# A hybrid decoder layer on one core: 16 of the 22 up steps of each feed-forward computed as seven block products

## The chip, the cores and the metric
The kernel runs on one core of one Trainium2 chip. The metric is the device time of one launch in microseconds; the time before is 1206.61 us, the median of three runs (1205.77 to 1208.55).

## The reference
The layer is a feed-forward, a token mixer and a second feed-forward, each between RMS norms, for 512 tokens of width 1024. The change touches only the feed-forwards:

```python
def rms_norm(x, g):
    xf = x.astype(jnp.float32)
    y = xf * lax.rsqrt(jnp.mean(xf * xf, axis=-1, keepdims=True) + EPS)
    return (y * g.astype(jnp.float32)).astype(x.dtype)
...
def swiglu(x, w_gu, w_down):
    g, u = jnp.split(x @ w_gu, 2, axis=-1)
    return (jax.nn.silu(g) * u) @ w_down
```

Here w_gu is 1024 by 5632 (2816 gate columns, 2816 up columns) and w_down is 2816 by 1024, all float32.

## The kernel before
**Work and tiles.** One feed-forward is 22 up steps and 11 down steps. An up step takes 128 gate and 128 up columns of w_gu, 1 MB of weights, as 8 row blocks of 256 columns, and multiplies them with the normed x, held transposed (`xn`, 8 blocks of 128 rows by 512 tokens). A down step takes 256 rows of w_down, also 1 MB.

**Precision.** Every float32 operand is split into a rounded part (hi) and the rest (lo), and a product is three matmuls: hi by hi, hi by lo, lo by hi (`MODES`). So an up step is 8 blocks, 2 output tiles and 3 modes, 48 matmuls of 128x128 by 512 columns; a down step is 48 as well.

**The weight ring.** SyncE's queue loads step n into `ring_raw` slot n % 2, as two transfers of 512 KB (`load`). ACT copies it to `ring_hi` (`hi`, L670), VectorE subtracts to give `ring_lo` (`lo`, L946) and signals `lo_ready`; the load of step n waits until `lo` of step n-2 is done. ACT's copy waits for the matmuls of step n-2 (`w_used`), since there are two slots of `ring_hi` and `ring_lo`.

**After an up step**, VectorE multiplies gate and up sums by the norm's factor `rb` (L1024, L1025), ACT takes the silu (L734), VectorE multiplies (L1028), ACT rounds (L738) and VectorE subtracts (L1033), which gives `hT_hi` and `hT_lo` for the down steps. Each engine runs its instructions in the order of the program, and a wait holds all that is behind it on that engine.

**GpSimd (POOL)** builds the attention bias tables while the first up steps run: a memset and copies into `bias_vec` (L551, L560), a store (L563), five broadcasts to DRAM (L571); later it adds y to x (`add_x`, L585).

## Time and profile before

| what | value |
|---|---|
| median of 3 runs | 1206.61 us |
| profiled execution, device time | 1207.43 us |
| its span in the trace | 1205.7 us |
| PE busy / VectorE / ACT / POOL | 99% / 44% / 33% / 7% |
| granted TensorE clock, mean | 0.999 |
| data moved | 123.19 MB, mean 102 GB/s |

The time of the profiled execution is 1.7 us more than its span. "Busy" of PE counts overlapping matmuls once; the pitch of matmuls is read from the start of one to the start of the next, or from a piece of the chain divided by its count, not from the duration of one.

### The profile page before, as it was taken

What the parts mean: (1) busy time and instruction counts of PE and PEld (TensorE: products, weight loads), DVE (VectorE), ACT (ScalarE), POOL (GpSimd) and SP (SyncE); (2) the same over time, 40 slices, a digit from 0 to 9 for tenths busy, and PEclk for the clock granted to TensorE, in tenths of its full rate; (3) what the DMA queues carried; (4) which work ended last, traced back from release to release, by engine and by line L of the source; (5) the groups of instructions that cost most, each with busy time, mean ns of one, the idle gap of its engine ahead of it and who ended that gap; (6) DMA issues with size and microseconds to landing.
All of it is one profiled execution on the core that took longest, in us unless ns stands there. A gap on an engine that the chain in (4) does not pass through costs nothing.

```text
span 1205.7 us, 15537 instructions
## 1 busy us (share of the span) xinstructions
PE 1188.7 (99%) x6054; PEld 986.2 (82%) x6054; DVE 535.2 (44%) x806; ACT 399.0 (33%) x643; POOL 86.8 (7%) x198
## 2 busy tenths in 40 slices
PE   9999999999999999999999999999999999999998
PEld 7888888888887888998777788887888888888886
DVE  3444444431226435436776343646444444442223
ACT  5222222221125211246676313325422222221113
POOL 7000000000005100000031100002000000000002
PEclk9999999999999999999999999999999999999999
DMA  7843333232225343371200232332333333333321
GB/s 207 263 113 96 104 104 87 87 123 105 105 87 145 96 118 104 108 242 36 73 3 2 70 105 70 123 105 70 101 90 88 104 104 96 83 115 107 105 70 70
DMA packets 138511, 123.19 MB, mean 102 GB/s; under 512 B 4180, under 2 KB 125180, under 8 KB 138444
## 3 DMA queue, kind: packets, MB, share of 16 engines
q1 hardware_dynamic: 134272, 108.02, 29.7%
q0 software_dynamic: 4080, 14.50, 3.7%
q8 instruction: 32, 0.52, 0.2%
q14 instruction: 15, 0.12, 0.0%
q10 hardware_dynamic: 112, 0.03, 0.0%
HBM read 118.08 MB, written 8.90 MB: 105 GB/s over the span
## 4 chain that ended last, share of the span: by engine, by line
PE 93%; DVE 2%; DMA 2%; ACT 1%; issue 1%; SPq 0%; DVEq 0%; ACTq 0%
PE ps L1369 53%; PE ps L1453 20%; PE ps L1556 4%; PE ps L1824 4%; PE ps L1622 2%; PE ps L1611 2%; DMA ring_raw<-in_ffn_w_gu 2%; PE ps L1808 2%; PE ps L1679 2%; PE ps L1657 1%; PE ps L1796 1%; PE ps L1393 1%; ACT ring_hi L670 1%; DVE ring_lo L946 1%; DMA x_tok<-in_x 0%
## 5 line engine op out<-in xcount | busy, mean ns | idle before, releaser
L1369 PE MATMUL ps<-xn_hi,ring_hi 128*128 128x512 f32 x992 | 388.7, 392 | 2.9 <-DVE ring_lo L946 1.6
L1369 PE MATMUL ps<-xn_hi,ring_lo 128*128 128x512 f32 x992 | 386.2, 389 | 0.0
L1369 PE MATMUL ps<-xn_lo,ring_hi 128*128 128x512 f32 x992 | 386.1, 389 | 0.0
L946 DVE TENSOR_TENSOR ring_lo<-ring_raw,ring_hi 128x2048 fp32r<-128x2048 f32 (+1 forms) x89 | 201.8, 2268 | 255.5 <-ACT ring_hi L670 255.5
L670 ACT ACTIVATE ring_hi<-ring_raw 128x2048 fp32r<-128x2048 f32 (+1 forms) x89 | 167.9, 1888 | 255.1 <-PE ps L1453 157.6
L1369 PEld LDWEIGHTS ps<-xn_hi,ring_hi 128*128 128x128 f32 x992 | 186.2, 188 | 42.7 <-issue 4.3
L1369 PEld LDWEIGHTS ps<-xn_hi,ring_lo 128*128 128x128 f32 x992 | 186.2, 188 | 39.1
L1369 PEld LDWEIGHTS ps<-xn_lo,ring_hi 128*128 128x128 f32 x992 | 186.3, 188 | 37.7
L1453 PE MATMUL ps<-ring_hi,hT_hi 128*128 128x512 f32 x352 | 136.9, 389 | 0.0
L1453 PE MATMUL ps<-ring_hi,hT_lo 128*128 128x512 f32 x352 | 136.9, 389 | 0.0
L1453 PE MATMUL ps<-ring_lo,hT_hi 128*128 128x512 f32 x352 | 136.9, 389 | 0.0
L734 ACT ACTIVATE silu_g<-silu_g 128x512 f32<-128x512 f32 x44 | 27.8, 632 | 324.4 <-DVE silu_g L1024 324.4
L1024 DVE TENSOR_TENSOR silu_g<-ps,rb 128x512 f32<-128x512 f32 x44 | 30.4, 691 | 187.1 <-PE ps L1369 187.0
L1453 PEld LDWEIGHTS ps<-ring_hi,hT_lo 128*128 128x128 f32 x352 | 66.1, 188 | 13.8
L1453 PEld LDWEIGHTS ps<-ring_hi,hT_hi 128*128 128x128 f32 x352 | 66.1, 188 | 13.7
L1453 PEld LDWEIGHTS ps<-ring_lo,hT_hi 128*128 128x128 f32 x352 | 66.1, 188 | 13.7
L957 DVE TENSOR_TENSOR ring_lo<-ring_raw,ring_hi 128x1024 fp32r<-128x1024 f32 x22 | 26.0, 1221 | 51.2 <-ACT ring_hi L680 51.1
L585 POOL TENSOR_TENSOR x_tok<-y_gained,x_tok 128x512 f32<-128x512 f32 x18 | 22.7, 1281 | 291.2 <-DVE y_gained L999 291.2
L836 ACT ACTIVATE p_n<-s_sb,stat_m 128x128 f32<-128x128 f32 (+2 forms) x64 | 35.3, 552 | 18.4 <-DVE stat_m L1175 18.4
L1556 PE MATMUL ps<-ring_hi,xn_hi 128*128 128x256 f32 x128 | 36.5, 285 | 0.7 <-DVE ring_lo L957 0.7
L680 ACT ACTIVATE ring_hi<-ring_raw 128x1024 fp32r<-128x1024 f32 x22 | 22.1, 1051 | 44.3 <-PE ps L1556 16.1
L1556 PE MATMUL ps<-ring_lo,xn_hi 128*128 128x256 f32 x128 | 36.2, 283 | 0.0
(232 smaller groups left out, 1161.6 us busy)
## 6 DMA issues: line engine op xcount, KB each, us to landing
ring_raw<-in_ffn_w_gu SPq DMA_DIRECT2D x86, 512.0 KB, 5.0
ring_raw<-in_ffn_w_down SPq DMA_DIRECT2D x44, 512.0 KB, 4.0
ring_raw<-in_w_in SPq DMA_DIRECT2D x44, 512.0 KB, 4.7
ring_raw<-in_w_out SPq DMA_DIRECT2D x8, 512.0 KB, 4.3
bias_rows_sparse<-bias_by_distance POOLq DMA_DIRECT2D x1, 2560.0 KB, 15.5
x_tok<-in_x SPq DMA_DIRECT2D x8, 256.0 KB, 5.3
ring_raw<-in_cmp_w_k SPq DMA_DIRECT2D x4, 512.0 KB, 4.4
ring_raw<-in_cmp_w_v SPq DMA_DIRECT2D x4, 512.0 KB, 4.5
```

The costliest lines, as they stand in the source:

```text
L670: e = act.activation(dst, src, ACT.Copy)
L734: act.activation(silu_g[:, u, :], silu_g[:, u, :], ACT.Silu).then_inc(act_read, 1)
L836: e = act.activation(p_of(u)[:, c0:c1], s_sb[:, u % 2, c0:c1], ACT.Exp, bias=least, scale=-1.0, accum_out=den)
L946: e = dve.tensor_tensor(dst, src, f32(r), ALU.subtract)
L957: return dve.tensor_tensor(dst, src, f32(r), ALU.subtract)
L1024: dve.tensor_tensor(silu_g[:, u, :], ps[:, 2 * slot, :], rb[:, :], ALU.mult).then_inc(g_scaled, 1)
L1369: e = pe.matmul(ps[:, 2 * (slot if pair is None else pair) + c, :], part(a, slot, k * 256 + c * P, P), xn[b][:, k, :], start=(k == 0 and i ...
L1453: e = pe.matmul(ps[:, j, :], hT[b][:, tokens], part(a, ring_slot(n0), kk * D + c * S, S), start=(n == 0 and kk == 0 and q == 0), stop=(n = ...
L1556: e = pe.matmul(ps[:, V_BANK[i][t // 2], (t % 2) * 256:(t % 2) * 256 + 256], xn[b][:, k, tokens], part(a, ring_slot(n), k * 256, 256), sta ...
L1611: e = pe.matmul(ps[:, (u + half) % 4, c0:c1], q, k, start=True, stop=True)
L1622: e = pe.transpose(ps[:, 4 + u % 2, x * P:x * P + P], p_of(u)[:, x * P:x * P + P], ident[:, :])
L1824: e = pe.matmul(ps[:, 2 * t + c, :], xn[b][:, k, t * P:t * P + P], part(a, ring_slot(n), kk * D + c * S, S), start=(k == 0 and q == 0), st ...
```

## The change
An up step's product is a 2 by 2 block product: X is cut into X11, X12 (tokens 0 to 255, upper and lower half of the 1024 rows) and X21, X22 (tokens 256 to 511); W into B11, B12, B21, B22 (upper and lower half of the rows by gate and up columns). Strassen's identity in Winograd's form needs seven block products instead of eight: of X11, S1, S2, X12, S3, X22, S4 with B11, T1, T2, B21, T3, T4, B22. Steps 0 to 5 of each feed-forward (`CLASSIC`) stay as they were; steps 6 to 21 (`MIXED`) become block products, each of 4 row blocks by 3 modes, 12 matmuls of 128x128 by 256 columns, 84 in a step.

The S blocks are made once in each feed-forward by VectorE (`join_x`, `norm_x`, `mix_x`, `lo_mixed`), with `rb` multiplied in; ACT rounds them (`hi_mixed`). The T blocks are made anew in each step by POOL (`mix_weights`, four tensor_tensor of 128x512). ACT and VectorE split the seven weight blocks one by one (`hi_block`, `lo_block`, 128x512 each). The product of B11 goes into bank x and is copied by ACT into bank y (`seed`); ACT also takes two partial sums to SBUF (`z_part`, `t_part`), which VectorE adds (`c22`, `c12`). The rounding of h moves into the down steps (`hi_h`, `lo_h`), and POOL's work on the bias tables moves behind the up steps of the first feed-forward. The loads and their waits are as before.

```diff
-PAIR_PROJ = UP
+CLASSIC = 6
+MIXED = UP - CLASSIC
+BLOCKS = ("B11", "T1", "T2", "B21", "T3", "T4", "B22")
+B11, T1, T2, B21, T3, T4, B22 = range(7)
+X11, S1, S2, X12, S3, X22, S4 = range(7)
+PAIR_PROJ = CLASSIC
...
+            def mix_weights(f, i, u):
+                b11, b12, b21, b22 = [ring_raw[:, u % 2, :].rearrange("p (k c) -> p k c", c=256)[:, k0:k0 + 4, c0:c0 + P]
+                                      for k0 in (0, 4) for c0 in (0, P)]
+                t1, t2, t3, t4 = [weights_of(f, u, b) for b in (T1, T2, T3, T4)]
+                begins = isinstance(i, int) and 2 * i + u == 0
+                pool.wait_ge(raw_loaded[u % 2], raw_count(f, i, u))
+                if not begins:
+                    pool.wait_ge(blk_lo[T1], of_step(f, i, u, 0))
+                pool.tensor_tensor(t1, b12, b11, ALU.subtract).then_inc(t_ready[T1], 1)
+                if not begins:
+                    pool.wait_ge(blk_lo[T3], of_step(f, i, u, 0))
+                pool.tensor_tensor(t3, b22, b12, ALU.subtract).then_inc(t_ready[T3], 1)
+                if not begins:
+                    pool.wait_ge(blk_lo[T2], of_step(f, i, u, 0))
+                pool.wait_ge(t_ready[T3], of_step(f, i, u))
+                pool.tensor_tensor(t2, t3, b11, ALU.add).then_inc(t_ready[T2], 1)
+                pool.wait_ge(*((w_used, base_of(f)) if begins else (blk_lo[T4], of_step(f, i, u, 0))))
+                pool.wait_ge(t_ready[T2], of_step(f, i, u))
+                pool.tensor_tensor(t4, b21, t2, ALU.subtract).then_inc(t_ready[T4], 1)
+            def mix(f):
+                for u in range(2):
+                    mix_weights(f, 0, u)
+                with pool.Fori(1, MIXED // 2) as i:
+                    for u in range(2):
+                        mix_weights(f, i, u)
+                pool.wait_ge(up_scaled, CLASSIC * (f + 1))
...
+            mix(0)
+            load_gain(g1_post)
+            pool.wait_ge(w_used, UP)
+            pool.memset(bias_vec[0:20, :], MASKED).then_inc(vec_filled, 1)
...
+                def seed(i, u):
+                    x, y = [ps[:, bank, 0:256] for bank in CORNERS[u % 2][:2]]
+                    act.wait_ge(blk_used[B11], of_step(f, i, u))
+                    if isinstance(i, int) and 2 * i + u < 2:
+                        act.wait_ge(up_scaled, CLASSIC * f + CLASSIC - 1 + u)
+                    act.activation(y, x, ACT.Copy).then_inc(y_seeded, 1)
+                def mixed(i, u, ahead=7, late=lambda: None, later=lambda: None):
+                    x, y, z = [ps[:, bank, 0:256] for bank in CORNERS[u % 2]]
+                    def following(b):
+                        if ahead > 1:
+                            hi_block(i, u + 1, b)
+                    act.wait_ge(blk_used[T1], of_step(f, i, u))
                     if not (isinstance(i, int) and 2 * i + u == 0):
-                        hi(i, base + u + 2)
-                    act.wait_ge(h_ready, 2 * i + (h0 + u + 1))
-                    act.activation(hT_hi[:, bass.ds(i * (2 * S) + u * S, S)], h_f32[:, u, :], ACT.Copy).then_inc(hhi_ready, 1)
+                        act.wait_ge(c22_taken, of_step(f, i, u, 0))
+                    act.activation(z_part[:, :], z, ACT.Copy).then_inc(z_taken, 1)
+                    following(T1)
+                    act.wait_ge(blk_used[T2], of_step(f, i, u))
+                    if not (isinstance(i, int) and 2 * i + u == 0):
+                        act.wait_ge(c12_taken, of_step(f, i, u, 0))
+                    act.activation(t_part[:, :], y, ACT.Copy).then_inc(t_taken, 1)
+                    late()
+                    following(T2)
+                    if ahead == 1:
+                        hi_down(0)
+                    act.wait_ge(blk_used[B21], of_step(f, i, u))
+                    act.wait_ge(h_ready, 2 * i + (UP * f + CLASSIC + u - 1))
+                    act.activation(silu_g[:, u % 2, 0:256], x, ACT.Silu).then_inc(silu_ready, 1)
+                    if ahead == 1:
+                        hi_down(1)
+                    following(B21)
+                    following(T3)
+                    later()
+                    if ahead > 1:
+                        seed(i, u + 1)
+                    if ahead > 2:
+                        hi_block(i, u + 2, B11)
+                    act.wait_ge(blk_used[T4], of_step(f, i, u))
+                    act.activation(silu_g[:, u % 2, 256:512], y, ACT.Silu).then_inc(silu_ready, 1)
+                    following(T4)
+                    following(B22)
...
+                def lo_block(i, u, b):
+                    if b < 6:
+                        dve.wait_ge(blk_hi[b], of_step(f, i, u))
+                    else:
+                        dve.wait_ge(hi_ready, 2 * i + (base_of(f) + u + 1))
+                    dve.tensor_tensor(by_tile(block_at(1, f, b)), weights_of(f, u, b), f32(by_tile(block_at(0, f, b))),
+                                      ALU.subtract).then_inc(blk_lo[b] if b < 6 else lo_ready, 1)
...
+                def mixed(i, u, ahead=7, late=lambda: None, later=lambda: None):
+                    v = u % 2
+                    _, y, z = [ps[:, bank, 0:256] for bank in CORNERS[v]]
+                    def following(b):
+                        if ahead > 1:
+                            lo_block(i, u + 1, b)
+                    following(T1)
+                    late()
+                    following(T2)
+                    if ahead == 1:
+                        lo_half_of(first_down, 0, (2, 5 + 2 * NV)[f]).then_inc(w_half, 1)
+                    dve.wait_ge(blk_used[T3], of_step(f, i, u))
+                    dve.wait_ge(z_taken, of_step(f, i, u))
+                    dve.tensor_tensor(h_f32[:, v, 256:512], y, z_part[:, :], ALU.add).then_inc(c22_taken, 1)
+                    later()
+                    if ahead == 1:
+                        lo_half_of(first_down, 1, 0).then_inc(lo_ready, 1)
+                    following(B21)
+                    following(T3)
+                    if ahead > 2:
+                        lo_block(i, u + 2, B11)
+                    dve.wait_ge(w_used, 2 * i + (base_of(f) + u + 1))
+                    dve.wait_ge(t_taken, of_step(f, i, u))
+                    dve.tensor_tensor(h_f32[:, v, 0:256], z, t_part[:, :], ALU.add).then_inc(c12_taken, 1)
+                    dve.wait_ge(silu_ready, of_step(f, i, u, 2, 2))
+                    dve.wait_ge(c22_taken, of_step(f, i, u))
+                    dve.wait_ge(c12_taken, of_step(f, i, u))
+                    at_j = bass.ds(i * (2 * S) + (CLASSIC + u) * S, S)
+                    dve.tensor_tensor(hT[:, at_j], silu_g[:, v, :], h_f32[:, v, :], ALU.mult).then_inc(h_ready, 1)
+                    following(T4)
+                    following(B22)
...
+                def product(i, u, b):
+                    starting = isinstance(i, int) and 2 * i + u == 0
+                    starts = isinstance(i, int) and 2 * i + u < 2
+                    x, y, z = CORNERS[u % 2]
+                    bank = {B11: x, T1: z, T2: y, B21: x, T3: y, T4: y, B22: z}[b]
+                    if b < 6:
+                        pe.wait_ge(blk_lo[b], of_step(f, i, u))
+                    else:
+                        pe.wait_ge(lo_ready, 2 * i + (base_of(f) + u + 1))
+                    if starting:
+                        pe.wait_ge(sx_lo, 7 * f + X_ORDER.index(b) + 1)
+                    if b == B11:
+                        pe.wait_ge(*((up_scaled, CLASSIC * f + CLASSIC - 1) if starts else (silu_ready, of_step(f, i, u - 2, 1, 2))))
+                    if b == T1 and not starts:
+                        pe.wait_ge(c12_taken, of_step(f, i, u - 2))
+                    if b == T2:
+                        pe.wait_ge(y_seeded, of_step(f, i, u))
+                    if b == T3:
+                        pe.wait_ge(t_taken, of_step(f, i, u))
+                    if b == T4:
+                        pe.wait_ge(c22_taken, of_step(f, i, u))
+                    if b == B22:
+                        pe.wait_ge(z_taken, of_step(f, i, u))
+                    for k in range(4):
+                        for q, (a, x) in enumerate(MODES):
+                            e = pe.matmul(ps[:, bank, 0:256], block_at(a, f, b)[:, k * P:(k + 1) * P], (x_hi, x_lo)[x][b][:, k, :],
+                                          start=(b in (B11, T1) and k == 0 and q == 0), stop=(k == 3 and q == 2), skip_group_check=True)
+                    e.then_inc(blk_used[b] if b < 6 else w_used, 1)
+                def mixed(i, u, last=False):
+                    for b in (T1, T2, B21, T3):
+                        product(i, u, b)
+                    if not last:
+                        product(i, u + 1, B11)
+                    for b in (T4, B22):
+                        product(i, u, b)
```

Three places in the order of the instructions. First, VectorE in its loop over up steps. Before, one up step (`h_f` is the up half and then the product, `rb` the norm's factor):

```order
L1021 REGISTER_ALU [waits w_used]
L1024 TENSOR_TENSOR silu_g<-ps,rb 128x512 [waits hlo_ready,hhi_ready,h_ready]
L1025 TENSOR_TENSOR h_f_60<-ps,rb 128x512
L1028 TENSOR_TENSOR h_f_60<-silu_g,h_f_60 128x512 [waits up_scaled,act_read]
L940 REGISTER_ALU
L946 TENSOR_TENSOR ring_lo<-ring_raw,ring_hi 128x2048 [waits hi_ready]
L1033 ISA [waits hhi_ready]
L1033 TENSOR_TENSOR hT_lo<-h_f_60,hT_hi 128x512
```

Now, the second part of one mixed step, from B21 of the next step to its B22 (`b21_hi` and the like are ACT's signals for a rounded block, `hi_ready` that for B22):

```order
L1278 TENSOR_TENSOR ring_lo<-ring_raw,ring_hi 128x512 [waits b21_hi]
L1278 TENSOR_TENSOR ring_lo<-t_raw,ring_hi 128x512 [waits t3_hi]
L1275 REGISTER_ALU
L1278 TENSOR_TENSOR ring_lo<-ring_raw,ring_hi 128x512 [waits b11_hi]
L1313 TENSOR_TENSOR h_f_90<-ps,t_part 128x256 [waits t_taken,w_used]
L1314 REGISTER_ALU
L1318 ISA [waits c12_taken,c22_taken,silu_ready]
L1318 TENSOR_TENSOR hT<-silu_g,h_f_90 128x512
L1278 TENSOR_TENSOR ring_lo<-t_raw,ring_hi 128x512 [waits t4_hi]
L1277 REGISTER_ALU
L1278 TENSOR_TENSOR ring_lo<-ring_raw,ring_hi 128x512 [waits hi_ready]
```

The one subtraction over a whole step's weights has become seven; that of B11 belongs to the step after next and stands ahead of those of T4 and B22 of the next step.

Second, POOL behind its first constants. Before, the bias tables come at once:

```order
L550 DMA tab<-in_rel_bias 20x32
L551 MEMSET bias_vec 20x2560
L556 TENSOR_SCALAR neg_tab<-tab 20x32
L560 COPY bias_vec<-neg_tab 20x62
L560 COPY bias_vec<-neg_tab 20x118
```

Now the loop of the weight mixes stands there, two steps in a turn (`t_raw` are the four buffers for T blocks; `t1_lo` is VectorE's signal that T1 of the step before is split):

```order
L645 TENSOR_TENSOR t_raw<-ring_raw 128x512 [waits t1_lo]
L648 TENSOR_TENSOR t_raw<-ring_raw 128x512 [waits t3_lo]
L651 REGISTER_ALU [waits t2_lo]
L652 TENSOR_TENSOR t_raw<-t_raw,ring_raw 128x512 [waits t3_summed]
L655 TENSOR_TENSOR t_raw<-ring_raw,t_raw 128x512 [waits t2_summed,t4_lo]
L645 TENSOR_TENSOR t_raw<-ring_raw 128x512 [waits t1_lo,raw_loaded1]
L648 TENSOR_TENSOR t_raw<-ring_raw 128x512 [waits t3_lo]
```

The bias tables (now L668 on) follow behind the loop and a wait for `w_used` of step 21.

Third, ACT in the middle of a mixed step. Before, its loop holds three instructions a step:

```order
L734 ACTIVATE silu_g<-silu_g 128x512 [waits g_scaled]
L666 ISA
L670 ACTIVATE ring_hi<-ring_raw 128x2048 [waits w_used,raw_loaded0]
L738 ISA [waits h_ready]
L738 ACTIVATE hT_hi<-h_f_60 128x512
```

Now, from the seed of the next step to that step's B22:

```order
L874 ACTIVATE ps<-ps 128x256 [waits b11_used]
L851 REGISTER_ALU
L853 ACTIVATE ring_hi<-ring_raw 128x512 [waits b11_used,raw_loaded0]
L910 ACTIVATE silu_g<-ps 128x256 [waits t4_used]
L853 ACTIVATE ring_hi<-t_raw 128x512 [waits t4_used,t4_summed]
L852 REGISTER_ALU [waits raw_loaded1]
L853 ACTIVATE ring_hi<-ring_raw 128x512 [waits w_used]
```

The copy of B11 of the step after next waits for that step's load (`raw_loaded0`) and stands ahead of the copies of T4 and B22 of the next step.

## Rows read from the trace of the kernel before

**Rows 1.** The page: busy time (part 1), granted clock (part 2).
```profile
PE 1188.7 (99%) x6054; PEld 986.2 (82%) x6054; DVE 535.2 (44%) x806; ACT 399.0 (33%) x643; POOL 86.8 (7%) x198
...
PEclk9999999999999999999999999999999999999999
```

**Rows 2.** The chain that ended last, in order of time: start us, us, what.
```profile
33.22 22.68 DMA ring_raw<-in_ffn_w_gu
55.92 1.92 ACT ring_hi L670
57.87 2.30 DVE ring_lo L946
60.30 196.13 PE ps L1369 x864
256.43 119.69 PE ps L1453 x528
...
514.40 8.63 PE ps L1556 x72
...
528.22 11.51 PE ps L1556 x96
```

**Rows 3.** Groups by line and shape: busy us, mean ns of one | idle before, releaser.
```profile
L946 DVE TENSOR_TENSOR ring_lo<-ring_raw,ring_hi 128x2048 fp32r<-128x2048 f32 x87 | 199.4, 2292 | 254.6 <-ACT ring_hi L670 254.6
...
L1028 DVE TENSOR_TENSOR h_f<-silu_g,h_f 128x512 f32<-128x512 f32 x44 | 30.5, 692 | 6.3 <-ACT silu_g L734 3.8
...
L738 ACT ACTIVATE hT_hi<-h_f 128x512 f32 x40 | 24.4, 611 | 0.0
L957 DVE TENSOR_TENSOR ring_lo<-ring_raw,ring_hi 128x1024 fp32r<-128x1024 f32 x22 | 26.0, 1221 | 51.2 <-ACT ring_hi L680 51.1
L585 POOL TENSOR_TENSOR x_tok<-y_gained,x_tok 128x512 f32<-128x512 f32 x18 | 22.7, 1281 | 291.2 <-DVE y_gained L999 291.2
...
L1175 DVE CUSTOM_DVE_ANT_0 s_sb<-ps,bias_n 128x256 f32<-128x256 f32 x16 | 5.9, 420 | 0.5 <-ACT p_n L836 0.5
```

**Rows 4.** Timeline of SyncE's queue at 196.8 us: start us, us, engine, instruction.
```profile
196.83 1.00 SPq L447 DMA_DIRECT2D ring_raw<-in_ffn_w_gu  x2
```

**Rows 5.** Timeline of VectorE from 194 us.
```profile
194.38 2.29 DVE L946 TENSOR_TENSOR ring_lo<-ring_raw,ring_hi 128x2048 fp32r<-128x2048 f32 x1 [1.11 <-ACT ring_hi L670]
196.59 0.69 DVE L1033 TENSOR_TENSOR hT_lo<-h_f,hT_hi 128x512 f32 x1
202.25 0.69 DVE L1024 TENSOR_TENSOR silu_g<-ps,rb 128x512 f32<-128x512 f32 x1 [4.98 <-PE ps L1369]
202.86 0.68 DVE L1025 TENSOR_TENSOR h_f<-ps,rb 128x512 f32<-128x512 f32 x1
```

**Rows 6.** The page, part 6: KB each, us from issue to landing.
```profile
ring_raw<-in_ffn_w_gu SPq DMA_DIRECT2D x86, 512.0 KB, 5.0
```

**Rows 7.** Timeline from 667.5 us, VectorE and POOL.
```profile
668.02 2.28 DVE L946 TENSOR_TENSOR ring_lo<-ring_raw,ring_hi 128x2048 fp32r<-128x2048 f32 x1
668.25 3.19 POOL L621 TENSOR_TENSOR y_nsa<-y_nsa,o_tmp 128x512 f32<-128x512 f32 x1 [12.44 <-DVE o_tmp L1226]
```

**Rows 8.** Timeline from 1193 us, POOL and VectorE.
```profile
1199.36 2.50 POOL L585 TENSOR_TENSOR x_tok<-y_gained,x_tok 128x512 f32<-128x512 f32 x2 [0.18 <-DVE y_gained L999]
...
1201.52 0.89 DVE L1012 SCALAR_TENSOR_TENSOR x_tok<-y_gained,y_rstd,x_tok 128x512 f32<-128x512 f32 x1
```

**Rows 9.** Timeline from 614 us, POOL and, beside it, VectorE.
```profile
614.27 1.27 POOL L621 TENSOR_TENSOR y_nsa<-y_nsa,o_tmp 128x512 f32<-128x512 f32 x1 [26.61 <-DVE o_tmp L1226]
...
614.39 0.42 DVE L1175 CUSTOM_DVE_ANT_0 s_sb<-ps,bias_n 128x256 f32<-128x256 f32 x1
```

**Rows 10.** Timeline of POOL: the bias tables, and the first add of y to x.
```profile
7.66 16.07 POOL L560 COPY bias_vec<-neg_tab 20x62 f32<-20x62 f32 x107
24.04 0.59 POOL L563 DMA_DIRECT2D bias_by_distance<-bias_vec  x1 [0.30 <-POOL bias_vec L560]
...
30.10 1.05 POOL L571 DMA_DIRECT2D bias_rows_compressed<-bias_by_distance  x1
...
370.30 5.04 POOL L585 TENSOR_TENSOR x_tok<-y_gained,x_tok 128x512 f32<-128x512 f32 x4 [111.37 <-DVE y_gained L999]
```

More of the change, by code:

```diff
@@ L656, in _ @@
             add_x(1)
-            pool.wait_ge(up_scaled, 2 * UP)
+            mix(1)
             load_gain(g2_post)
@@ L776, in _ @@
             root()
-            ffn(FFN1, 0, 0, 0)
+            ffn(FFN1, 0, 0)
             for m in range(KD):
@@ L1140, in _ @@
                 if MIX + step + 2 <= GATE:
-                    lo_halves(MIX + step + 2, step + 4)
+                    lo_halves(MIX + step + 2, step + 5)
                 if kind == "v":
@@ L1458, in down @@
                     e.then_inc(w_used, 1)
+                for n in range(CLASSIC):
+                    up(n)
+                product(0, 0, B11)
                 for u in range(2):
-                    up(0, u)
-                with pe.Fori(1, UP // 2) as i:
+                    mixed(0, u)
+                with pe.Fori(1, MIXED // 2 - 1) as i:
                     for u in range(2):
-                        up(i, u)
-                pe.wait_ge(hlo_ready, h0 + UP - 2)
-                for n in range(DOWN - 1):
+                        mixed(i, u)
+                for u in range(2):
+                    mixed(MIXED // 2 - 1, u, last=u == 1)
+                for n in range(DOWN):
                     down(n)
-                pe.wait_ge(hlo_ready, h0 + UP)
-                down(DOWN - 1)
             pe.wait_ge(consts, 5)
```

334 lines of the change are left out of this document (247 added, 87 removed).

## The prediction
> **What bounds the kernel now.** The page comes first: PE is busy for 99% of the span, VectorE for 44%, POOL for 7%, and PE has its full clock in all slices [rows 1]. The chain of waits says the same: nearly all of it is PE working through its steps [rows 2]. So time can only come from fewer or shorter matmuls, or be lost by making PE wait. The durations of matmuls (389 ns) overlap; the pitch is what counts. The chain gives it: 864 matmuls of 512 columns in 196.13 us, 0.2270 us each, and 528 of the down steps in 119.69 us, the same. For 256 columns there are two clean pieces, 72 in 8.63 us and 96 in 11.51 us, 0.1199 us each [rows 2]. An up step is 48 x 0.2270 = 10.90 us, and everything that another engine does in a step has to fit in that.
>
> **What the change takes off PE.** A mixed step is 84 matmuls of 256 columns, 84 x 0.1199 = 10.07 us, 0.83 less than 10.90. Half the columns cost 53% of the pitch, so of the 12.5% saved in arithmetic 7.6% are left. The form is that of the measured pieces: 128x128 stationary, 256 columns moving. Thirty-two steps give 26.4 us. I cost the more frequent waits on PE at nothing where they are already met: in 864 matmuls with a wait at each step the mean pitch shows no surcharge [rows 2]. From both sides: 0, or the 0.2 us that a late signal costs, at 7 waits a step 1.4 us a step; the unbroken piece is nearer to 0.
>
> **What it adds on the other engines**, a step. ACT: seven copies of 128x512 at 0.61 [rows 3], and five short operations. Those of 128x256 are not in the trace for a copy; from above they cost 0.61, from below half of that, 0.3. That is 5.8 to 7.3 us of 10.07, and fits. VectorE: seven subtractions of 128x512 and one product of that size, 0.69 each [rows 3], pitch 0.61 where nothing is waited for (202.25 to 202.86 [rows 5]), and two adds of 128x256 with a PSUM operand, 0.42 like that of L1175 [rows 3]: about 6.2 us. POOL: four tensor_tensor of 128x512 at 1.28 [rows 3], 5.1 us. Each alone fits. Two things make it not fit.
>
> **First, the loop through the load.** The load of step s+2 waits until VectorE has split B22 of step s; call that moment R(s). In the order of the instructions the split of B11 of step s+2 stands ahead of the c12 add, the product h, and the splits of T4 and B22 of step s+1, and the last of these is R(s+1). So each R waits for the one before plus a whole load. The load: the SyncE queue issues 0.16 us after VectorE's end (196.67 to 196.83 [rows 4, 5]), the second half about 0.5 later (two issues take 1.00), and a half takes 5.0 us to land [rows 6]: 5.7 us. Then ACT's copy of B11, 0.04 + 0.61, VectorE's split, 0.04 + 0.69; c12, 0.34 after overlap; h, which waits for c12, 0.04 + 0.69; T4 and B22, 0.61 each. That is 3.7 us, and R(s+1) - R(s) = 9.4 us: under PE's 10.07, by 0.7 us. Before, the same loop had only to close within 10.90, with its load landing many microseconds ahead of its use: VectorE idled 254.6 us ahead of L946 for ACT, which itself was waiting for PE's slots [rows 3].
>
> **Second, POOL and VectorE get in each other's way, and just there.** At 668.02 VectorE ran L946, whose inputs are both in SBUF; POOL's add started at 668.25 and took 3.19 us where 1.28 is usual. It ended at 671.44, 1.14 after VectorE's end at 670.30: it had stood still meanwhile [rows 7]. The other way round, POOL's last add ended at 1201.86, and a VectorE instruction with two SBUF inputs begun at 1201.52 took 0.89 and ended 0.55 after POOL [rows 8]. With one input in PSUM nothing of this is seen: at 614 POOL's add took 1.27 beside VectorE's 0.42s [rows 9]. The Trainium skill, SBUF — State Buffer, section Who interferes with whom, states this as a rule: a VectorE instruction with two SBUF inputs and a GpSimd one that reads SBUF exclude each other, and the second to issue is blocked until the first is done. The trace agrees (3.19 against 1.28); without the rule the forecast would be the first rival below, with it the likeliest case. So each POOL mix holds VectorE's splits and h off for 1.14 us, and each of these holds POOL off for 0.55.
>
> The mixes of step s+2 start at the very moment that its load lands, as does ACT's copy of B11. With the landing as zero: POOL makes T1 until 1.35. VectorE wants to split B11 at 0.7, is let in at 1.35, and ends at 1.9. T3, next on POOL, runs from 1.9 to 3.0; c12 (PSUM) is done by 2.25, h stands until 3.0 and ends at 3.55. T2 waits since about 3.3. If the two engines then take turns, T2 goes to 4.7, the split of T4 to 5.25, that of B22, already queued, to 5.85. The loop is 5.7 + 5.85 = 11.55 us. If VectorE keeps its turn, T4 and B22 follow h at once and end at 4.8: 10.5 us. No row shows POOL waiting behind two such VectorE instructions in a row. The ends for this cost are 3.7 (POOL never in the way) and, with POOL first each time, 6.0 (T1, T3 to 2.6, B11 3.15, T2 4.3, h 4.85, T4 and B22 6.05). I take 5.85, since both rows show that an engine that waits is served within a few hundredths of the other's end.
>
> **The sum.** With the end of step 5 as zero. The first mixed step has extra work on VectorE: X22, S4 (1.22 each, as L957 [rows 3]) and six blocks, with four mixes between. Added up in order, B22 of the first mixed step is split at R = 10.9. (Nothing in the way: 8.4.) PE's T4 product of that step waits for the c22 add behind the split of T2 of the next, until 12.0 where its own pace has it at 8.6. From there 14 turns of 11.55 (the last load with a mix is that of the sixteenth mixed step): 172.6. After that no load is waited for: c22 of step 20 comes 2.65 us after (T4's mix, two splits, the add), its T4 and B22 products 2.9, four products of step 21 5.75, c22 0.7, the last two products 2.9: 15.0, so 187.6. Before, sixteen steps were 16 x 10.90 = 174.4. That is +13.2 for one feed-forward, +26.4 for two.
>
> The bias tables move to the down steps of the first feed-forward. POOL's part took from 7.7 to 31 us, the broadcasts up to 24 us more; now they start near 270 us and have 100 us until POOL is needed at 370.3 [rows 10]. But their traffic stretches a weight load: 22.68 us in place of 5, and the step behind it then started as its split ended [rows 2]. This happens again, with ACT and VectorE 1.0 and 1.2 us a step busier for h: 0 to 3 us, I take 1. If POOL were late for the add, each us would count in full.
>
> Hidden, each with its cover: making the S blocks is 8 operations of 1.22 in VectorE ahead of the splits of x, at most 6.1 us between two steps on top of 2.1 and 2.3 [rows 3], 10.5 of 10.9; if it spills over, step 5's weights, due 10.9 later, still come in time. The split of h is 1.0 and 1.2 us in down steps of 10.9 us where ACT and VectorE have 1.9 and 2.3 to do.
>
> 1207.4 + 26.4 + 1 = 1234.8 us for an execution like the profiled one, which is 0.8 above the median of the runs: **1234 us**.
>
> **Rivals.**
> - *The other sign: PE sets the pace.* If the mixes don't hold VectorE up on the loop (it is let in, or the load lands sooner), the loop is 9.4 and PE's 10.07 decides. Then 26.4 us come off, less 1.4 us twice for the late first c22, plus 1: 1207.4 - 22.6 = 1184.8, median 1184. It decides below a loop of 10.07, that is if POOL costs the loop less than 0.7 us. Against it: T1 alone, begun with the landing, costs 0.65, and T3 another 0.75. 14%.
> - *VectorE keeps its turn.* Loop 10.5: R starts at 10.0, 14 turns 147.0, end 13.9, so 170.9, which is 3.5 less than 174.4; two of them and the bias work: 1207.4 - 7 + 1 = 1201.4, median 1201. Speaks for it: its instructions stand ready one behind another, the gap between them is under 0.1. 20%.
> - *POOL costs more*: it goes first each time, or its mixes on strided blocks are slower than a contiguous add. Each 0.1 us in the loop is 2.8 us; 0.2 to 0.6 more give 1240 to 1251. 11%.
> - The likeliest, turns taken: 55%.
>
> **Numbers.** The likeliest alone: 1224 to 1246 (its loop 11.2 to 11.9). For 8 in 10 the range has to reach nearly to the first rival: 1187 to 1249. A measurement of this kernel tells 0.2%, 2.4 us, from no change. Faster: 14% and most of the 20%, 30% together. Within 0.2%: 6%. Slower: 64%.
>
> **What the profile after would show.** (1) Matmuls of 256 columns at pitch 0.120 inside a product. (2) The mixed steps 11.5 us apart, PE idle about 1.4 us in each ahead of the T4 product, waiting for VectorE's c22 add. (3) VectorE's 128x512 subtractions with a mean well over 0.69, POOL's mixes over 1.28. (4) ACT's copy of B11 waiting for the load, in most steps. (5) POOL's add at the end of the first feed-forward on time. I am wrong if ACT's B11 copies find their load landed (rival one), or if the turns go to VectorE: then splits of T4 and B22 lie 0.61 apart with a POOL mix of 2 us or more beside them.

## The result and the profile after

The changed kernel takes 1244.52 us (median of 4 runs, 1243.62 to 1246.15) against 1206.19 for the kernel before on the same chip: ratio 1.0316, interval 1.0297 to 1.0335. It is slower by 38 us. The profiled execution has a span of 1241.9 us, 36.2 more than before.

The page of the kernel after, parts 1 and 2, to be held against [rows 1]:
```profile
PE 1173.7 (95%) x7206; PEld 1025.8 (83%) x7206; DVE 723.5 (58%) x1016; ACT 506.8 (41%) x957; POOL 298.3 (24%) x326
...
PEclk9998999999999999999999999999999999999999
```
PE is busy 15.0 us less than before and the span is 36.2 us longer, so PE now idles for 68 us in place of 17. No other engine is busy for more than 58%. This is a kernel that waits, and the chain says for what.

The chain of the kernel after, in order of time (start us, us, what):
```profile
32.46 49.01 PE ps L1695 x216
...
93.17 5.08 DMA ring_raw<-in_ffn_w_gu
104.97 5.00 DMA ring_raw<-in_ffn_w_gu
...
246.30 5.06 DMA ring_raw<-in_ffn_w_gu
261.19 8.88 PE ps L1792 x72
270.67 3.10 PE ps L1792 x24
273.77 119.72 PE ps L1822 x528
...
935.26 5.22 DMA ring_raw<-in_ffn_w_gu
...
1088.95 5.10 DMA ring_raw<-in_ffn_w_gu
```
Before, this stretch was one piece of PE, 864 matmuls long [rows 2]. Now the chain holds 14 loads in the 16 mixed steps of the first feed-forward, (246.30 - 93.17) / 13 = 11.78 us apart, and in the second (1088.95 - 935.26) / 13 = 11.82. The first feed-forward's mixed steps last from 81.47 to 273.77, 192.3 us where it was 174.4.

The 8 in the row of the clock is the start of those steps. PE and, below it, a stretch of five microseconds (busy us and instructions of PE, PEld, DVE, ACT, POOL, then granted clock, DMA share, GB/s):
```profile
93.53 0.55 PE L1792 MATMUL ps<-x_hi,ring_hi 128*128 128x256 f32 x1 [3.44 <-DVE h_f L1303]
```
```profile
93.50:98.50 5.00, 4.97 (x23) 5.00 (x24) 2.97 (x5) 1.22 (x3) 0.09 (x1) 0.50 0.75 210
```
PE had idled for 3.44 us, and for the next five its granted clock was 0.50, the lower of its two levels (1.2 GHz), with matmuls 0.213 us apart; from 99.2 on they are 0.120 apart again. The turn in which this falls lasts 104.97 - 93.17 = 11.80 us, as the others: PE doesn't set the pace here, so the slow stretch costs nothing.

The waits of the kernel after (engine, what waited, for what: us, times, longest):
```profile
ACT ring_hi L853 <- DMA ring_raw<-in_ffn_w_gu: 114.0, 28, 4.6
PE ps L1792 <- DVE h_f L1303: 51.5, 32, 3.4
ACT ring_hi L853 <- POOL t_raw L652: 39.6, 30, 1.9
```
and its groups by line and shape:
```profile
L1278 DVE TENSOR_TENSOR ring_lo<-t_raw,ring_hi 128x512 fp32r<-128x512 f32 x128 | 149.3, 1185 | 12.3 <-ACT ring_hi L853 12.3
...
L1278 DVE TENSOR_TENSOR ring_lo<-ring_raw,ring_hi 128x512 fp32r<-128x512 f32 x96 | 86.0, 896 | 74.4 <-ACT ring_hi L853 74.4
...
L648 POOL TENSOR_TENSOR t_raw<-ring_raw 128x512 f32<-128x512 f32 x32 | 57.1, 1783 | 0.0
```
A split of 128x512 that takes 0.69 alone takes 1.185 in the mean for a T block and 0.896 for a B block, and POOL's T3 mix takes 1.783 where 1.28 is usual.

One turn of the loop, timelines of the kernel after: VectorE,
```profile
193.25 1.31 DVE L1278 TENSOR_TENSOR ring_lo<-ring_raw,ring_hi 128x512 fp32r<-128x512 f32 x1 [2.81 <-ACT ring_hi L853]
194.49 0.41 DVE L1313 TENSOR_TENSOR h_f<-ps,t_part 128x256 f32<-128x256 f32 x1
195.15 1.12 DVE L1318 TENSOR_TENSOR hT<-silu_g,h_f 128x512 f32 x1 [0.25 <-DVE h_f L1313]
196.20 1.77 DVE L1278 TENSOR_TENSOR ring_lo<-t_raw,ring_hi 128x512 fp32r<-128x512 f32 x1
197.90 0.68 DVE L1278 TENSOR_TENSOR ring_lo<-ring_raw,ring_hi 128x512 fp32r<-128x512 f32 x1
198.50 2.38 DVE L1278 TENSOR_TENSOR ring_lo<-t_raw,ring_hi 128x512 fp32r<-128x512 f32 x2
200.80 0.41 DVE L1303 TENSOR_TENSOR h_f<-ps,z_part 128x256 f32<-128x256 f32 x1
```
POOL,
```profile
192.72 1.30 POOL L645 TENSOR_TENSOR t_raw<-ring_raw 128x512 f32<-128x512 f32 x1 [4.96 <-DMA ring_raw<-in_ffn_w_gu]
193.96 1.76 POOL L648 TENSOR_TENSOR t_raw<-ring_raw 128x512 f32<-128x512 f32 x1
195.80 1.62 POOL L652 TENSOR_TENSOR t_raw<-t_raw,ring_raw 128x512 f32<-128x512 f32 x1
198.05 1.68 POOL L655 TENSOR_TENSOR t_raw<-ring_raw,t_raw 128x512 f32<-128x512 f32 x1 [0.63 <-DVE ring_lo L1278]
```
and PE:
```profile
201.36 0.36 PE L1792 MATMUL ps<-x_hi,ring_hi 128*128 128x256 f32 x1 [1.67 <-DVE h_f L1303]
```
Read the ends in turn. The load landed at 192.57. POOL's T1 ends at 194.02, VectorE's B11 split at 194.56, POOL's T3 at 195.72, VectorE's h at 196.27, POOL's T2 at 197.42, VectorE's T4 split at 197.97: each VectorE end is 0.55 behind POOL's, each POOL end 1.15 behind VectorE's. B22, which starts when no mix is running, takes 0.68, and its end at 198.58 is R. From landing to R 6.01 us, and PE's T4 product starts at 201.36 after waiting 1.67.

### The profile page after: what moved, and what is told of

Same layout as the page of the kernel before. It is cut to its first block, busy times and chain, and to the rows that moved or that the text cites. A ratio compares the mean times of both kernels' runs of the same rounds, so it can differ in the third digit from the quotient of the medians.

```text
span 1241.9 us, 18963 instructions
## 1 busy us (share of the span) xinstructions
PE 1173.7 (95%) x7206; PEld 1025.8 (83%) x7206; DVE 723.5 (58%) x1016; ACT 506.8 (41%) x957; POOL 298.3 (24%) x326
## 4 chain that ended last, share of the span: by engine, by line
PE 66%; DMA 12%; DVE 11%; issue 6%; ACT 2%; SPq 1%; DVEq 1%; ACTq 0%
PE ps L1695 26%; PE ps L1822 19%; DMA ring_raw<-in_ffn_w_gu 12%; DVE ring_lo L1278 7%; PE ps L1927 4%; PE ps L2195 4%; PE ps L1993 2%; PE ps L1982 2%; PE ps L1792 2%; PE ps L2179 2%; PE ps L2050 2%; ACT ring_hi L853 2%; SPq L515 1%; PE ps L2028 1%; DVE h_f L1313 1%
## 5 line engine op out<-in xcount | busy, mean ns | idle before, releaser
L1695 PE MATMUL ps<-xn_hi,ring_hi 128*128 128x512 f32 x480 | 189.5, 395 | 2.7 <-DVE ring_lo L1149 1.4
L1695 PE MATMUL ps<-xn_hi,ring_lo 128*128 128x512 f32 x480 | 187.1, 390 | 0.0
L1695 PE MATMUL ps<-xn_lo,ring_hi 128*128 128x512 f32 x480 | 186.9, 389 | 0.0
L1792 PE MATMUL ps<-x_hi,ring_hi 128*128 128x256 f32 x384 | 112.1, 292 | 51.5 <-DVE h_f L1303 51.5
L1278 DVE TENSOR_TENSOR ring_lo<-t_raw,ring_hi 128x512 fp32r<-128x512 f32 x128 | 149.3, 1185 | 12.3 <-ACT ring_hi L853 12.3
L1792 PE MATMUL ps<-s_hi,ring_hi 128*128 128x256 f32 x512 | 145.8, 285 | 0.0
L1792 PE MATMUL ps<-s_lo,ring_hi 128*128 128x256 f32 x512 | 145.7, 285 | 0.0
L1792 PE MATMUL ps<-s_hi,ring_lo 128*128 128x256 f32 x512 | 145.6, 284 | 0.0
L1822 PE MATMUL ps<-ring_hi,h_hi 128*128 128x512 f32 x352 | 137.0, 389 | 0.0
L1822 PE MATMUL ps<-ring_lo,h_hi 128*128 128x512 f32 x352 | 136.9, 389 | 0.0
L853 ACT ACTIVATE ring_hi<-ring_raw 128x512 fp32r<-128x512 f32 x96 | 59.9, 624 | 115.2 <-DMA ring_raw<-in_ffn_w_gu 114.0
```

The source lines that it names most:

```text
L853: act.activation(by_tile(block_at(0, f, b)), weights_of(f, u, b), ACT.Copy).then_inc(blk_hi[b] if b < 6 else hi_ready, 1)
L1278: dve.tensor_tensor(by_tile(block_at(1, f, b)), weights_of(f, u, b), f32(by_tile(block_at(0, f, b))), ALU.subtract).then_inc(blk_lo[b] if ...
L1695: e = pe.matmul(ps[:, 2 * (slot if pair is None else pair) + c, :], part(a, slot, k * 256 + c * P, P), xn[b][:, k, :], start=(k == 0 and i ...
L1792: e = pe.matmul(ps[:, bank, 0:256], block_at(a, f, b)[:, k * P:(k + 1) * P], (x_hi, x_lo)[x][b][:, k, :], start=(b in (B11, T1) and k == 0 ...
L1822: e = pe.matmul(ps[:, j, :], tokens[b], part(a, ring_slot(n0), kk * D + c * S, S), start=(n == 0 and kk == 0 and q == 0), stop=(n == DOWN ...
```

## The experiments

Each ratio is against the kernel before on the same chip. The medians of that kernel lie between 1206.2 and 1208.0 us on the chips used, so a difference between two experiments can be off by up to 2 us. A kernel's line numbers differ by a few from those of the kernel after. "R" is the end of VectorE's B22 split, as in the prediction.

### 1. The B11 block behind B22
ACT's copy and VectorE's split of B11 of the step after next move behind T4 and B22, so that nothing ahead of R waits for a load:
```diff
                     following(T4)
                     following(B22)
+                    if ahead > 2:
+                        lo_block(i, u + 2, B11)
```


> ACT and VectorE take B11 of the step after next behind T4 and B22 of the next step, and nothing else changes. Theory A (the loop through the load sets the pace, 11.8 us a step in the changed kernel, and VectorE and POOL holding each other off only stretches it): with the load out of the loop, PE or the two engines' summed time decides, 10.1 to 10.7 us a step, so about 28 x 1.1 to 1.7 = 30 to 48 us less than 1244, 1197 to 1214 us. Theory B (the exclusion of VectorE and POOL alone saturates the pair, 8 x 0.55 + 4 x 1.14 + two adds and gaps, wherever B11 stands): 11 to 11.8 us a step, 1222 to 1244 us.

1230.53 us, ratio 1.0189 (1.0172 to 1.0206): faster than the kernel after by 14 us, far from A's 1197 to 1214 and within B's 1222 to 1244. Taking the load out of the loop was not enough; what stood in its place is in the trace. PE, then VectorE:
```profile
183.83 0.38 PE L1792 MATMUL ps<-x_hi,ring_hi 128*128 128x256 f32 x1 [0.87 <-DVE ring_lo L1278]
```
```profile
188.53 0.42 DVE L1311 TENSOR_TENSOR h_f<-ps,t_part 128x256 f32<-128x256 f32 x1 [2.10 <-PE ps L1792]
...
189.81 1.79 DVE L1278 TENSOR_TENSOR ring_lo<-t_raw,ring_hi 128x512 fp32r<-128x512 f32 x1
191.53 3.47 DVE L1278 TENSOR_TENSOR ring_lo<-ring_raw,ring_hi 128x512 fp32r<-128x512 f32 x2
```
B11 is now the last of five operations behind the end of a step (c12, h, T4, B22, B11), and PE's B11, T4 and B22 products of the next step wait for it: a loop of one step, 4.7 us on PE and 6.6 on VectorE, 11.30 in all. Three splits of about 1.74 in place of 0.61 make it so long: at 0.61 it would be 7.9 and bind nothing. So B had the time and the stretching right, but not that the two engines have no time left: VectorE idles 2.10 us ahead of c12 in each of these steps, waiting for PE.

### 2. The mixes on POOL cut to 4 columns
```diff
                     for u in range(2):
-                        mix_weights(f, i, u)
+                        mix_weights(f, i, u, 4)
```
From step 8 on the T blocks keep most of what they held; the output is not the layer's.

> POOL's four mixes in the loop are made on 4 instead of 128 columns of each row block (the T blocks of steps 8 to 21 are left mostly as they were, so the output isn't the layer's); all waits and the order stay. Theory A: the loop falls to what is left without the mixes, 5.85 for the load and 3.9 for the rest, 9.8 us, under PE's 10.07, so PE sets the pace: 1244 less 28 x 1.7 = 1196 us, less about 2 of the start, 1185 to 1197 us. A rival in which the load alone (or its wait in ACT's order) sets the pace whatever POOL does: no change, 1240 us or more.

1192.48 us, ratio 0.9872 (0.9855 to 0.9888), within A. With order, waits and loads as in the kernel after, 52 us go with POOL's work alone. No load is on the chain any more, and the later steps of the first feed-forward are 10.08 us apart, PE's pace. What it still loses is mostly at the start of each feed-forward, where the mixes are whole: the mixed steps last 168.4 and 167.2 us where sixteen of 10.07 are 161.1. PE starts at 93.87 after a wait for c22, at clock 0.50 as above, and the first 28 matmuls take 6.08 us where 0.1199 each gives 3.36: here, where PE sets the pace, the low clock costs 2.7 us.

### 3. Is it POOL's result that is late, or VectorE's turn?
The kernel of 2, with a 128x512 addition on POOL behind each narrow mix, on a buffer that nobody reads in that time (same output remark):
```diff
                 pool.tensor_tensor(t1, b12, b11, ALU.subtract).then_inc(t_ready[T1], 1)
+                pool.tensor_tensor(gain_rows[:, S:D], gain_rows[:, S:D], gain_rows[:, S:D], ALU.add).then_inc(spare_done, 1)
```


> The kernel e2_narrow (mixes of 4 columns from step 8 on, output not the layer's), in which each narrow mix is followed by an addition of 128x512 on POOL, in a buffer that nobody reads or waits for. Theory A (VectorE waits for its turn at the memory that POOL holds): the additions take VectorE's time as the mixes did, steps of 11.3 to 11.8 us, 1230 to 1246 us. Theory B (what cost the time in the kernel after is that ACT and VectorE wait for POOL's results): nobody waits, 1192 to 1200 us.

1233.12 us, ratio 1.0224 (1.0207 to 1.0241): 41 us more than experiment 2, for work that no instruction waits for except POOL's own. The groups of this kernel:
```profile
L648 POOL TENSOR_TENSOR gain_rows<-gain_rows 128x512 f32<-128x512 f32 x112 | 141.0, 1259 | 0.0
L1292 DVE TENSOR_TENSOR ring_lo<-t_raw,ring_hi 128x512 fp32r<-128x512 f32 x128 | 111.0, 886 | 12.3 <-ACT ring_hi L867 12.3
L1292 DVE TENSOR_TENSOR ring_lo<-ring_raw,ring_hi 128x512 fp32r<-128x512 f32 x96 | 107.5, 1120 | 79.4 <-ACT ring_hi L867 79.4
```
The splits stretch again, to 886 and 1120 ns; its loads are 11.4 us apart on the chain. The additions also delay POOL's own next mix, and ACT waits for T2 because of it, but only 12.5 us in 28 steps (39.6 in the kernel after), and no piece of the chain in the mixed steps from 100 to 250 us is POOL's. So the time goes by VectorE's turns with POOL and not by data that come late.

### 4. Less to load
From step 8 on the second transfer of each load, with b12 and b22, carries 8 of 128 columns, the rest keeps older weights (not the layer's output):
```diff
-                     (v[:, :, P:256], by_k(w_gu[:, bass.ds(i * (2 * P) + (u * P + F), P)])))
+                     (v[:, :, P:P + w], by_k(w_gu[:, bass.ds(i * (2 * P) + (u * P + F), w)])))
```


> The kernel after, but from step 8 on the second transfer of a step's weights (the half with the columns of b12 and b22) carries 8 of 128 columns; the rest of these blocks keeps the weights of earlier steps, so that the output is not the layer's. Theory A (the step is a loop through the load, the B11 copy and split, the end of the step, and the T4 and B22 splits, lengthened by turns with POOL): the load shrinks from 5.1 to some 2.7 us and the loop from 11.8 to some 9.5 us; then it no longer sets the pace, PE's 10.07 us with some waits for collisions does: steps of 10.3 to 10.9 us, 1202 to 1219 us in all. Theory B (VectorE's turns with POOL fill the step by themselves, whatever the load takes): steps of 11.4 us or more, 1234 to 1246.

1206.99 us, ratio 1.0004 (0.9995 to 1.0014), within A's range, though not as A has it. The chain:
```profile
124.66 3.83 DMA ring_raw<-in_ffn_w_gu
...
229.32 3.84 DMA ring_raw<-in_ffn_w_gu
```
Ten turns of 10.47 us. The load's piece shrank from about 5.1 to 3.8 and each turn by 1.31, the same: the load is on the loop with its full length. A had the load at 2.7 us and PE setting the pace with some waits; the load took 3.8 and the loop still sets it, and that both come to nearly the same time is luck. Half the bytes take three quarters of the time here, but in as many packets: 2080 in a step, as in the kernel after, of which 1056 are now under 512 bytes where 32 were.

### 5. Two of the four mixes on VectorE
T1 and T3 stay on POOL, T2 and T4 go behind R on VectorE:
```diff
                     following(T4)
                     following(B22)
+                    if ahead > 2:
+                        for b in (T2, T4):
+                            mix_t(i, u + 2, b)
```


> The kernel after with the mixes T1 and T3 on POOL and T2 and T4 on VectorE, behind the B22 split. Theory A (each mix of POOL's that meets a VectorE operation of the chain from the load to the B22 split makes the loop longer; those that meet nothing of it cost nothing): of the 11.8 us the T4 split's turn of 1.1 us goes and part of another, steps of 10.4 to 10.9, 1205 to 1219 us. Theory B (any 128x512 work of POOL's in the chain is enough to keep the pace near 11.8): 1235 or more. Theory C (the cost goes by the number of mixes on POOL, wherever they stand): half way between the 1197 of e4_mix_on_vector and 1244.5, 1221.

1209.44 us, ratio 1.0019 (1.0010 to 1.0029), within A, and 12 us below half way (C). VectorE in a turn:
```profile
183.85 1.12 DVE L1331 TENSOR_TENSOR hT<-silu_g,h_f 128x512 f32 x1 [0.25 <-DVE h_f L1326]
184.89 0.68 DVE L1272 TENSOR_TENSOR ring_lo<-t_raw,ring_hi 128x512 fp32r<-128x512 f32 x1
185.49 0.68 DVE L1272 TENSOR_TENSOR ring_lo<-ring_raw,ring_hi 128x512 fp32r<-128x512 f32 x1
```
The T4 split is 1.09 us shorter than in the kernel after (0.68 against 1.77), and the turns, 10.68 us, are 1.10 shorter. What counts is which VectorE operation of the loop a mix meets, not how many mixes there are.

### 6. The longest wait of PE, moved alone
In the kernel after VectorE adds c22, for which PE waits 51.5 us, ahead of the T2 split:
```diff
                     following(T1)
                     late()
-                    following(T2)
...
                     dve.tensor_tensor(h_f32[:, v, 256:512], y, z_part[:, :], ALU.add).then_inc(c22_taken, 1)
+                    following(T2)
```


> The kernel after with one edit: VectorE adds c22 ahead of the T2 split instead of behind it. PE's longest wait in the kernel after is that of the T4 product for this add, 51.5 us in all. Theory A (that wait is only where the loop's time shows; the loop from the load to the B22 split doesn't pass through the c22 add): PE waits elsewhere, the steps stay 11.6 to 11.8 us apart, 1239 to 1247. Theory B (the place of the add in the queue is the cause): the add comes 1.2 us earlier and the steps lose as much, 1208 to 1222.

1244.28 us, ratio 1.0311 (1.0288 to 1.0333): no change against the kernel after, within A. PE still waits 51.0 us for that add; that it would wait elsewhere was wrong. The loads are 11.79 us apart as before. A wait of the busiest engine names the place where the loop's surplus comes to light; c22 is a branch off the loop, and making a branch shorter gives nothing.

### 7. All mixes on VectorE
Behind R, in the order T1, T3, T2, T4, with B11 where the kernel after has it; POOL has nothing to do in a step:
```diff
+                    if ahead > 2:
+                        for b in (T1, T3, T2, T4):
+                            mix_t(i, u + 2, b)
```


> The four mixes of T blocks move from POOL to VectorE, all four behind B22 of the next step; B11 stays where the changed kernel has it, in the loop through the load. Nothing excludes anything now, and VectorE has 4 x 0.61 and some waits more, near 9.3 us a step in all. Theory A: loop 9.8 us, but the mixes stand ahead of the c22 add and so of PE's T4 product and of the end of the step that c12 waits for: 10.1 to 10.6 us a step, 1190 to 1210 us. If instead the loop through the load were 11.8 for a reason other than POOL, it stays at 1240.

1197.05 us, ratio 0.9909 (0.9893 to 0.9926), within A. Its groups:
```profile
L1273 DVE TENSOR_TENSOR ring_lo<-t_raw,ring_hi 128x512 fp32r<-128x512 f32 x128 | 85.0, 683 | 10.2 <-ACT ring_hi L848 10.2
...
L1291 DVE TENSOR_TENSOR t_raw<-ring_raw 128x512 f32<-128x512 f32 x64 | 41.3, 683 | 0.0
```
VectorE does eleven splits and mixes a step in place of seven splits, and is busy for 705.6 us, less than the 723.5 of the kernel after: four mixes of 0.69 cost it less than its turns with POOL's.

### 8. What is left over PE's pace
Steps in 7 are 10.28 us apart, PE's own pace is 10.07. Four kernels went after the rest, all with the mixes on VectorE. First with B11 behind B22, and the mixes T1, T3, T2 ahead of the c12 add:
```diff
                     following(T3)
+                    if ahead > 2:
+                        for b in (T1, T3, T2):
+                            mix_t(i, u + 2, b)
...
                     following(B22)
+                    if ahead > 2:
+                        lo_block(i, u + 2, B11)
+                        mix_t(i, u + 2, T4)
```


> Both: T1, T3, T2 of the step after next made by VectorE ahead of the c12 add, T4 and B11 behind B22; POOL has no part in the steps. Theory A: PE's own pace, 10.07 to 10.2 us a step, 1183 to 1190 us, faster than the kernel before. Theory B in a form without POOL (VectorE's time of about 9.3 us a step and its waits set the pace): 10.3 us or more a step and 1192 us or more.

1197.64 us, ratio 0.9919 (0.9902 to 0.9935), as 7: the gain expected of A didn't come, and the time is in B's range. But VectorE isn't short of time, it idles 1.8 us a step for the load. The chain:
```profile
121.48 5.08 DMA ring_raw<-in_ffn_w_gu
...
183.57 5.01 DMA ring_raw<-in_ffn_w_gu
```
Six turns of 10.35 us: the mixes ahead of c12 wait for a load, a loop of load, three mixes, c12, h, T4 and B22. This I overlooked at first. I saw that PE started each T4 product some 0.15 us late, behind a c22 add that stood behind splits. So c22 went ahead of the T2 split and the T4 mix, and the start of a feed-forward was put in the order that the expectation gives:
```diff
                     following(T1)
                     late()
-                    following(T2)
...
                     dve.tensor_tensor(h_f32[:, v, 256:512], y, z_part[:, :], ALU.add).then_inc(c22_taken, 1)
+                    following(T2)
+                    if ahead > 1:
+                        mix_t(i, u + 1, T4)
```


> The mixes on VectorE and the block B11 behind B22, as in e5_mix_vector_b11_last, but the c22 add of a step stands ahead of the T2 split and the T4 mix in VectorE's queue, and in the first mixed step the T4 and B22 splits stand ahead of S4's and the mixes of step 2 behind the end of the step. Theory A (what is left of a step over PE's 10.07 us in e5, 0.24 us, is one wait of the T4 product for the c22 add that stands behind splits; and each feed-forward's start loses some 4.5 us in four such waits): steps of 10.07 to 10.1 apart, 28 x 0.2 + 2 x 3 = 12 us less than 1197.6, so 1183 to 1189. Theory B (the 0.24 us are PE's own, at the border between products or at the loop's branch): 1190 to 1195.

1191.03 us, ratio 0.9872 (0.9856 to 0.9889), in B's range. The steps were no shorter: the loads on the chain are 10.37 us apart (119.40 to 171.24, five turns), so c22's new place gained nothing there. The gain is at the start: the c12 add of the first mixed step comes at 93.22 us in place of 96.59. Next the three mixes went behind B11, out of that loop:
```diff
-                    if ahead > 2 and not (isinstance(i, int) and 2 * i + u == 0):
-                        for b in (T1, T3, T2):
-                            mix_t(i, u + 2, b)
                     dve.wait_ge(w_used, 2 * i + (base_of(f) + u + 1))
```


> The kernel e6_c22_first with the mixes T1, T3 and T2 on VectorE behind the B22 and B11 splits in every step and not ahead of the c12 add, so that nothing that waits for a load stands ahead of the B22 split that starts the next one. Theory A (e6's 10.2 us a step are still a loop through the load: 5.65 from split to landed half, 1.9 for three mixes, 0.65 c12 to h, 0.6 each for h, T4 and B22 splits, 10.1 to 10.2 in all): the loop falls away and PE sets the pace, 10.07 to 10.1 us a step, 28 x 0.12 = 3.4 us less than 1191.0, 1186 to 1189. Theory B (the 0.13 us over PE's pace are PE's own): 1190 to 1192.

1206.51 us, ratio 0.9996 (0.9985 to 1.0007), outside both ranges. No load was on the chain any more, and there was a new wait. ACT in a step:
```profile
184.03 0.63 ACT L848 ACTIVATE ring_hi<-t_raw 128x512 fp32r<-128x512 f32 x1 [1.99 <-DVE t_raw L1291]
184.57 0.37 ACT L887 ACTIVATE t_part<-ps 128x256 f32<-128x256 f32 x1
```
and PE:
```profile
185.08 0.36 PE L1814 MATMUL ps<-s_hi,ring_hi 128*128 128x256 f32 x1 [0.58 <-ACT t_part L887]
```
The T1 copy waits 1.99 us for a mix that now comes later, and behind it in ACT's queue stands the t_part copy that PE's T3 product needs. I had looked only at VectorE's queue. The last kernel moves that one line:
```diff
                     act.activation(z_part[:, :], z, ACT.Copy).then_inc(z_taken, 1)
-                    following(T1)
...
                     act.activation(t_part[:, :], y, ACT.Copy).then_inc(t_taken, 1)
+                    following(T1)
```


> The kernel e10_none_ahead with ACT's copy of T1 behind its copy of the bank to t_part instead of ahead of it. In e10 PE waited 0.86 us a step in front of the T3 product for t_part, which stood in ACT's queue behind a T1 copy that waited 2.0 us for VectorE's T1 mix. Theory A (with that gone neither a load nor a mix stands ahead of anything that PE needs in a step): steps of 10.07 to 10.1 us, 28 x 0.8 = 22 us less than 1206.5, 1184 to 1189. Theory B (the T1 copy, now 2.5 us later than in e6_c22_first, makes T1's split or the c22 add late in its place): 1191 to 1200.

1184.20 us (1184.06 to 1185.08), ratio 0.9806 (0.9793 to 0.9819): it is in A's range and beats both kernels. Its chain in the first feed-forward:
```profile
80.63 4.33 PE ps L1814 x36
89.61 134.31 PE ps L1814 x1116
...
231.26 8.87 PE ps L1814 x72
240.73 3.10 PE ps L1814 x24
243.83 119.72 PE ps L1844 x528
```
1116 matmuls in 134.31 us, 0.1203 each, where the pitch inside a product is 0.1199: 93 products cost 0.5 us more in all, the drain of the last matmul and one late start included. The mixed steps last 163.2 us, where they were 174.4 before and 192.3 after. That also ends theory B of the two kernels before it (c22 first, and the mixes behind B11), that PE loses the rest by itself: its borders between products cost at most 5 ns each, and its steps are 10.08 us apart where 84 pitches are 10.07.

## Why the prediction was nearly right, and what it missed

The forecast was 1234, slower by turns of a loop through the load; measured were 1244.5, within the range. The change was forecast at 27.4 us and is 38.3. By its own steps:

| term, us | predicted | measured |
|---|---|---|
| pitch at 256 columns | 0.1199 | 0.120 |
| R of the first mixed step, after the end of step 5 | 10.9 | 11.0 |
| split to landing | 5.7 | 5.8 |
| landing to split | 5.85 | 6.01 |
| one turn | 11.55 | 11.78, 11.82 |
| from the last R to the down steps | 15.0 | 16.5 |
| one feed-forward's mixed steps | 187.6 | 192.3, 192.9 |
| bias tables, for the whole kernel | +1 | 0 |

(The first R: the split of B22 of the first mixed step runs from 90.70 to 92.45, less 81.47.)

- **PE.** As forecast: in the last kernel, which has the same matmuls, PE is busy for 1162.6 us, 26.1 less than before, where 26.4 were forecast. No surcharge for seven waits a step was right too; the 0.2 us at each wait taken as the upper end is refuted by the last kernel.
- **The loop.** Right where it was tried. Less to load shortens the turn by what the load shrinks (experiment 4), a link freed of POOL by 1.1 us (5). Experiment 1 qualifies it: with the load taken out, another loop of 11.3 us stood behind it, of the same stretched splits. The load decides where the time is lost, and POOL's whole mixes whether the loop is longer than PE's pace: without them, and with B11 in the same place, the kernel is at 1192 to 1197 (2, 7).
- **Turns.** As in [rows 7, 8], 0.55 and 1.15 us, and alternately. The rule of the Trainium skill that the prediction weighed (SBUF — State Buffer, section Who interferes with whom) holds here, with POOL's operations on a buffer of their own too (3). The rival that VectorE keeps its turn fell: the T4 split, ready behind h, ended 0.55 after POOL's T2. The c12 add, with inputs in PSUM and SBUF, takes 0.41 us in the middle of POOL's T3 mix and isn't held up.
- **The size of a turn** is the first term that was off, by 0.23 and 0.27 us: the load 0.07, T1's first end 0.10, handovers 0.06 (1.15 for 1.1 to 1.14). Over 28 turns that is 7.0 us of the miss.
- **The tail** is the second, 1.5 us twice. The prediction put the split of h among the hidden things, in the down steps. The first of them stands in the next to last mixed step, behind the T1 split and ahead of c22. VectorE there, in the kernel after:
```profile
258.90 1.21 DVE L1285 TENSOR_TENSOR hT_lo<-hT,h_hi 128x1024 fp32r<-128x1024 f32 x1
...
260.64 0.41 DVE L1303 TENSOR_TENSOR h_f<-ps,z_part 128x256 f32<-128x256 f32 x1
```
   The chain runs through both. The split of h takes 1.1 of the 1.5 us (from 258.90 to the next start at 260.04); the rest is in PE's last pieces and the starts behind c22.
- **The bias tables.** No load was stretched: the down steps take 119.72 us, before 119.69 [rows 2]. In return the first feed-forward's mixed steps begin 0.6 us sooner (81.47, where step 6 began at 82.09 before), and the load of 22.68 us [rows 2] is gone. POOL's add came on time: it is POOL that waits for VectorE there, 279.9 us over the six adds that wait.
- **The sum.** 7.0 for the turns, 3.0 for the tail and 0.2 for the start, less 1.6 for the bias tables' work and the earlier beginning, is 8.6; the span grew by 36.2 where 27.4 was forecast, 8.8 more. The bias tables' 1.6 us hide a part of the miss on the loop and the tail, 10.2.
- **The marks.** The five of the prediction are all in the profile: the pitch, the steps 11.8 apart with PE idle 1.5 to 1.7 ahead of T4, splits at 0.90 to 1.19 and mixes at 1.33 to 1.78, ACT's B11 copy waiting in 28 steps (114.0 us), the add on time.
- **The first rival**, PE sets the pace at 1184 if POOL doesn't hold the loop up, has the number of the last kernel, 1184.2, but not by its own condition. With nothing changed but POOL's work (experiment 2) the steps are at PE's pace and the kernel still takes 1192.5: a feed-forward's mixed steps last some 168 us, and the rival had 162.5, with 1.4 for the late first c22. To reach 1184 took, besides the mixes, four more changes of order: B11, the c22 add, the start of a feed-forward, ACT's T1 copy. Three of them were meant to cure a queue in which something wanted early stood behind something late; of these, the c22 add made the steps no shorter while a load was on their loop.

How the 0.55 us depends on size shows at one place in each feed-forward only, the split of X22, twice as wide. VectorE, then POOL, in the kernel after:
```profile
83.31 2.32 DVE L1270 TENSOR_TENSOR x_lo<-x,x_hi 128x1024 fp32r<-128x1024 f32 x1
```
```profile
82.79 1.76 POOL L645 TENSOR_TENSOR t_raw<-ring_raw 128x512 f32<-128x512 f32 x1
```
It ends 1.08 us behind POOL's mix and takes 1.22 alone; a split of 128x512 ends 0.55 behind and takes 0.69. So in both the operation that had to wait still needs its own length less 0.14 us. For other sizes, and for wider mixes on POOL, it stays open.

## What to carry to other kernels

Work moved to an idle engine isn't free when that engine and the one it relieves hold each other up, as POOL's mixes and VectorE's operations with two inputs in SBUF do here. Before giving POOL work beside VectorE, count the VectorE operations it will meet on a loop, and compare with letting VectorE do it (here 0.6 us each against 1.1 us a meeting). Where a wait of the busiest engine repeats in each step, look for the loop that closes it (here split, load, copy, split) and shorten a link of that; the wait itself may be on a branch. When an operation is moved in one engine's queue, go through what stands behind its readers in the other engines' queues as well.
